# Hybrid decoder step: attention tiles taken in reverse with new phases, and folded mLSTM weights

## The reference

```python
u = rmsnorm(x, pre_g) @ w_in            # 28 column tiles: QA KA VA ZA XB OB ZB, 4 heads each
# differential attention, 4 heads, two maps of 64 dims in each head
w = softmax(q1 k1^T / 8) - lam * softmax(q2 k2^T / 8);  a = headnorm(w @ v) * silu(za)
# mLSTM, 4 heads of 128; xc is a causal conv of 4 taps over xb
xch = silu(xc); qb = xch @ wq; kb = xch @ wk * 128**-0.5; vb = xb @ wv
gates = concat(qb, kb, vb) @ w_if + b_if
# chunked scan, stabilised: C = decay*C + sum wg * k (x) v ; n likewise
h = (w_in * q C + (q k^T * wD) v) / max(|den|, exp(-m)) * sigmoid(ob)
bo = (headnorm(h) + skip * xch) * silu(zb)
y = concat(a, bo) @ w_out; x = x + rmsnorm(y); x = x + rmsnorm(sigmoid(x@ple_gate) * (p@ple_w))
```

## Time and profile before

| | us |
|---|---|
| median of 3 runs (1136.88 to 1139.03) | 1138.99 |
| the profiled execution, its own time | 1136.47 |
| its span, first to last instruction | 1134.8 |
| TensorE busy in the span | 1009.9 (89%) |
| VectorE busy | 514.7 (45%) |
| ScalarE busy | 419.9 (37%) |
| mean granted TensorE clock | 0.961 of 2.4 GHz |

### The profile page before, as it was taken

One profiled execution on the slowest core, in us unless ns is written; L12 is line 12 of the kernel. 1 busy time (PEld: TensorE's weight loads), 2 busy tenths in 40 slices (PEclk: granted clock), 3 DMA queues, 4 the chain that ended last, 5 costly groups with the idle time before them and its releaser, 6 DMA issues.

```text
span 1134.8 us, 19697 instructions
## 1 busy us (share of the span) xinstructions
PE 1009.9 (89%) x7424; PEld 802.3 (71%) x7424; DVE 514.7 (45%) x1196; ACT 419.9 (37%) x902; POOL 137.1 (12%) x289
## 2 busy tenths in 40 slices
PE   4789999999999999985889888888876999899997
PEld 4779989999888888864556555555545888577773
DVE  4523744554653444433655545455443434432222
ACT  4433253333245434342544343344435223321111
POOL 1300010000000000030022222222220000000000
PEclk9989999999999999987999999899996999999998
DMA  6351115111322222239677666566365322212210
GB/s 195 88 149 57 57 57 131 56 57 57 103 75 79 71 75 61 71 91 282 202 240 243 205 207 222 182 217 219 117 235 209 143 95 75 82 48 84 83 66 24
DMA packets 111305, 142.16 MB, mean 125 GB/s; under 512 B 9304, under 2 KB 75481, under 8 KB 111212
## 3 DMA queue, kind: packets, MB, share of 16 engines
q1 hardware_dynamic: 100972, 107.34, 30.0%
q0 software_dynamic: 10240, 33.56, 9.4%
HBM read 125.47 MB, written 15.41 MB: 124 GB/s over the span
## 4 chain that ended last, share of the span: by engine, by line
PE 78%; DVE 9%; ACT 4%; issue 3%; DMA 3%; POOL 2%; SPq 1%; POOLq 0%; ACTq 0%; DVEq 0%
PE ps L1632 65%; PE ps L1635 12%; DVE pp L1508 2%; DMA out_k_prompt<-ktok 1%; DMA wst<-in_w_in 1%; DVE kTs L1456 1%; DMA xrow<-in_x_prompt 1%; DVE st L1506 1%; DVE pp L1495 1%; DVE hrow L1070 1%; DVE wlo L1076 1%; PE ps L1627 1%; SPq L366 1%; POOL si L666 1%; ACT whi L710 1%
## 5 line engine op out<-in xcount | busy, mean ns | idle before, releaser
L1632 PE MATMUL ps<-hhi,whi 128*128 128x272 f32 (+1 forms) x672 | 228.4, 340 | 6.8 <-DVE wlo L1076 5.6
L1632 PE MATMUL ps<-hhi,wlo 128*128 128x272 f32 (+1 forms) x672 | 219.2, 326 | 0.0
L1632 PE MATMUL ps<-hlo,whi 128*128 128x272 f32 (+1 forms) x672 | 218.4, 325 | 0.0
L1632 PE MATMUL ps<-wh,r 128*128 128x512 f32 (+1 forms) x576 | 163.6, 401 | 4.3 <-DVE wout_lo L1574 4.3
L1632 PEld LDWEIGHTS ps<-hhi,whi 128*128 128x128 f32 x672 | 129.0, 192 | 18.3 <-DVE wlo L1076 5.9
L1632 PEld LDWEIGHTS ps<-hlo,whi 128*128 128x128 f32 x672 | 129.1, 192 | 10.0 <-issue 1.9
L1632 PEld LDWEIGHTS ps<-hhi,wlo 128*128 128x128 f32 x672 | 128.6, 191 | 9.3
L1632 PEld LDWEIGHTS ps<-wh,r 128*128 128x128 f32 (+1 forms) x576 | 103.9, 183 | 33.8 <-issue 4.6
L1076 DVE TENSOR_TENSOR wlo<-wst,whi 128x1024 fp32r<-128x1024 f32 x56 | 68.6, 1224 | 87.7 <-ACT whi L710 87.7
L653 POOL DMA_DIRECT2D Vr<-in_cache_v x128 | 69.8, 545 | 206.0 <-PE ps L1632 186.3
L1456 DVE COPY kTs<-ps 128x512 f32<-128x512 f32 x64 | 44.3, 692 | 106.3 <-PE ps L1635 106.3
(11 more groups left out here) (305 smaller groups left out, 1602.7 us busy)
## 6 DMA issues: line engine op xcount, KB each, us to landing
Kr<-in_cache_k SPq DMA_DIRECT2D x128, 256.0 KB, 3.1
Vr<-in_cache_v POOLq DMA_DIRECT2D x128, 256.0 KB, 3.7
wst<-in_w_in SPq DMA_DIRECT2D x56, 512.0 KB, 3.8
out_y_prompt<-rows SPq DMA_DIRECT2D x16, 512.0 KB, 2.9
xrow<-in_x_prompt SPq DMA_DIRECT2D x8, 512.0 KB, 3.6
wout<-in_w_out SPq DMA_DIRECT2D x4, 1024.0 KB, 12.7
rows<-in_x_prompt SPq DMA_DIRECT2D x8, 512.0 KB, 4.3
wgate<-in_ple_gate_w SPq DMA_DIRECT2D x2, 2048.0 KB, 10.7
```

What stands on the lines that cost most here:

```text
L1632: return nc.tensor.matmul(out, lhsT, rhs, start=start, stop=stop)
```

## The change

The attention units are taken from the last tile of queries to the first (`tile_of`), so that units 0 to 15 have two parts and the others one; the phases of every engine are laid out anew; both maps' scores wait for the row minima of both and signal once. Decode steps are given out by the new sizes, the last five of them over positions of units 30 to 32. `ktok` has eight buffers, placed where `pp` lies later; the SiLU of ZA moves between the key tiles, and the state and sample outputs behind the eighth. In the mLSTM q and k are no longer both made: wq wk^T is folded once (`wqk`), x stands in k's place in the scores and the state, and wk is applied to the state at the end. The gate weights are folded too (`wg`, 8 blocks of 36 columns), and v is projected token-major at once. `wqk` and `wg` are copied to the second half's buffers by DMA.

```diff
-PARTS = [-(-(u // H + 1) * P // PART) for u in range(UNITS)]
+PARTS = [-(-(CH - u // H) * P // PART) for u in range(UNITS)]
...
+BUSY_UNITS = UNITS - 2
-SHARES = CH * [2.0] + [(4 + u // H) / PHASES if u < UNITS else 0.0 for u in range(UNITS + 4) for _ in range(PHASES)]
+SHARES = CH * [2.0] + [(4 + CH - u // H) / PHASES if u < BUSY_UNITS else 0.0 for u in range(UNITS + 4) for _ in range(PHASES)]
...
+DECODED = [round((STEPS_OF_DECODE - 5) * sum(SHARES[:pos + 1]) / sum(SHARES))
+           + min(5, max(0, (pos - CH - BUSY_UNITS * PHASES) // 2)) for pos in range(POSITIONS)]
...
+ktok = place("ktok", [P, CH, 512], offset=u1_base + XB * HALF * 4)
```

SP and ACT around the key tiles, and ACT's phases:

```diff
-            sp.wait_ge(s["C_done"], CH)
-            put("out_state", io["C_prompt"][0, 0].rearrange("h d e -> d h e"), Caug[:, :, 0:DH])
...
-                    sp.dma_start(kp[pos * P:(pos + 1) * P, :], ktok[:, pos % 2, :]).then_inc(k_out[pos % 2], 16)
+                    sp.dma_start(kp[pos * P:(pos + 1) * P, :], ktok[:, pos, :]).then_inc(k_out[pos // H], 16)
...
                 if pos == CH - 1:
+                    sp.wait_ge(*done["state_stored"])
+                    put("out_state", io["C_prompt"][0, 0].rearrange("h d e -> d h e"), Caug[:, :, 0:DH])
...
-            gate_tiles(ZA, 0, ACT.Silu)
-            gate_tiles(ZA, 1, ACT.Silu)
-            nc.scalar.preload_act_table_set("natural_log_exp_and_others")
             act.wait_ge(s["bo_done"], CH)
+            act.wait_ge(*done["state_ready"])
+            for b in range(2):
+                last = nc.scalar.activation(Caug[:, 2 * b:2 * b + 2, :].rearrange("p h d -> p (h d)"), ps[:, 6 + b, 0:258], ACT.Copy,
+                                            scale=KSCALE)
...
             def keys_out(t):
                 act.wait_ge(s["kt_ready"], t + 1)
-                if t >= 2:
-                    act.wait_ge(k_out[t % 2], 16 * (t // 2))
-                copy(ktok[:, t % 2, :], ps[:, 4 + t % 2, :], "kt_stored")
+                copy(ktok[:, t, :], ps[:, 4 + t % 2, :], "kt_stored")
+                if t == 2:
+                    gate_tiles(ZA, 0, ACT.Silu)
+                if t == 3:
+                    gate_tiles(ZA, 1, ACT.Silu)
...
             def attend(u, phase):
-                if phase == 0 and u >= 6 and u % H == 2:
-                    heads_square(u // H - 1)
+                if phase == 0 and two(u - 2):
+                    weights_out(u - 2, 1)
                 if phase == 1 and u < UNITS and not two(u):
                     head_exp(u)
-                if phase == 1 and 1 <= u <= UNITS:
+                if phase == 2 and u >= 5 and u % H == 1:
+                    heads_square(u // H - 1)
+                if phase == 3 and 1 <= u <= UNITS:
                     weights_out(u - 1, 0)
-                if phase == 2 and two(u - 1):
-                    weights_out(u - 1, 1)
                 if phase == 3 and two(u):
                     head_exp(u)
```

DVE and PE in the merged stage (DVE's `attend` keeps `head_rows(u, 0)` in phase 0, `head_weights(u - 1)` in phase 1 and `head_rows(u, 1)` in phase 2; `heads_scale` moves to phase 0):

```diff
             def head_rows(u, c):
+                if u < 2 and c == 0:
+                    dve.wait_ge(k_out[u], 16 * H)
...
+                dve.wait_ge(s["score_pair"], pair + 1)
                 for m in range(2):
...
-                    dve.wait_ge(s["score_pair"], 2 * pair + m + 1)
...
             def head_scores(u, c):
+                if pair:
+                    pe.wait_ge(s["row_min"], 2 * pair)
                 for m in range(2):
-                    if pair:
-                        pe.wait_ge(s["row_min"], 2 * pair - 1 + m)
...
             def attend(u, phase):
                 if phase == 0:
-                    if u >= 7 and u % H == 3:
-                        heads_back(u // H - 1)
                     if two(u):
                         head_scores(u, 1)
                     elif u + 1 < UNITS:
                         head_scores(u + 1, 0)
-                if phase == 1 and 1 <= u <= UNITS:
+                if phase == 1 and 2 <= u < UNITS + 2:
+                    head_values(u - 2)
+                if phase == 1 and u >= 7 and u % H == 3:
+                    heads_back(u // H - 1)
+                if phase == 2 and 1 <= u <= UNITS:
                     head_turn(u - 1, 0)
-                if phase == 2:
+                if phase == 3:
+                    if two(u) and u + 1 < UNITS:
+                        head_scores(u + 1, 0)
                     if two(u - 1):
                         head_turn(u - 1, 1)
-                    if two(u) and u + 1 < UNITS:
-                        head_scores(u + 1, 0)
-                if phase == 3 and 2 <= u < UNITS + 2:
-                    head_values(u - 2)
```

PE in the mLSTM: the folding, once, and the chunk:

```diff
-            fill(4)
+            fill(2)
...
+            for bank, w in ((6, wq), (7, wkv[:, 0, :, :]), (4, wkv[:, 1, :, :])):
+                for h in range(H):
+                    last = turn(ps[:, bank, h * P:(h + 1) * P], w[:, h, :])
+            last.then_inc(*signal["weights_T"])
+            fill()
...
+            for h in range(H):
+                mm(ps[:, 5, h * P:(h + 1) * P], qbT[:, h, :], kbT[:, h, :])
+            for h in range(H):
+                mm(ps[:, 6, 8 * h:8 * h + 8], qbT[:, h, :], wif[:, 3 * h, :], True, False)
+                mm(ps[:, 6, 8 * h:8 * h + 8], kbT[:, h, :], wif[:, 3 * h + 1, :], False, True)
+            for h in range(H):
+                last = mm(ps[:, 6, 32 + 8 * h:40 + 8 * h], wvT[:, h, :], wif[:, 3 * h + 2, :])
...
             def chunk(i):
...
-                for j in range(3):
...
-                    for h in range(H):
-                        src = tok(XB + h, i * P, P) if j == 2 else xch[:, h, t0:t0 + P]
-                        last = mm(ps[:, 4 + j, h * P:(h + 1) * P], wqkv[:, j, h, :], src)
-                    last.then_inc(s["proj_ready"], 1)
+                for h in range(H):
+                    last = mm(ps[:, 5, h * P:(h + 1) * P], wqk[:, h, :], x[h])
+                last.then_inc(s["proj_ready"], 1)
+                for h in range(H):
+                    last = turn(ps[:, 4, h * P:(h + 1) * P], x[h])
...
+                for h in range(H):
+                    last = mm(ps[:, 6, h * P:(h + 1) * P], tok(XB + h, i * P, P), wkv[:, 1, h, :])
...
+                for g in range(2 * H):
+                    last = mm(ps[0:36, 7, 0:P], wg[:, g, :], x[g] if g < H else tok(XB + g - H, i * P, P),
+                              g == 0, g == 2 * H - 1)
+                last.then_inc(s["gates_ready"], 1)
                 fill(before_turn)
                 if i % H:
                     finish(i - 1)
                 fill(before_gates)
-                pe.wait_ge(s["qk_stored"], 2 * i + 2)
+                pe.wait_ge(s["qk_stored"], i + 1)
                 pe.wait_ge(s["v_stored"], i + 1)
-                for c in range(12):
-                    for n in range(2):
-                        last = mm(ps[32 * n:32 * n + H, 7, 0:P], wif[:, c, H * n:H * n + H], (qbT, kbT, vbT)[c % 3][:, c // 3, :],
-                                  c == 0, c == 11)
-                last.then_inc(s["gates_ready"], 1)
-                for bank, buf in ((4, kbT), (5, vbT)):
-                    for h in range(H):
-                        last = turn(ps[:, bank, h * P:(h + 1) * P], buf[:, h, :])
...
+                    last = mm(ps[:, 6, h * P:(h + 1) * P], x[h], qbT[:, h, :])
...
             pe.wait_ge(s["C_done"], CH)
             pe.wait_ge(s["bo_done"], CH)
+            for h in range(H):
+                last = mm(ps[:, 6 + h // 2, 129 * (h % 2):129 * (h % 2) + 129], wkv_[1][:, 0, h, :], Caug[:, h, :])
+            last.then_inc(*signal["state_ready"])
```

More of the change, by code:

```diff
@@ L198, in program @@
         half_buffers.append(chunk_buffers(1, base))
[L199 to L200 removed]
+        end_of_chunks = base + 33856
+        assert top[0] <= end_of_chunks
+        E_, nd_, vaug_, qbT_, kw_, Ablk_, gat_, G_, wqk_, wkv_, xch_, wg_ = (
             [b[name] for b in half_buffers]
[L202 removed]
+            for name in ("E", "nd", "vaug", "qbT", "kw", "Ablk", "gat", "G", "wqk", "wkv", "xch", "wg"))
+        wvT = kw_[0]
         top[0] = sample_base
@@ L239, in program @@
         mask_w = place("mask_w", [P, SEQ])
-        ktok = place("ktok", [P, 2, 512])
         pT = place("pT", [P, PAGES + 1, 32])
@@ L243, in program @@
         S = [None, place("S1", [P, PAST + SMP])]
+        kS = place("kS", [SMP, 512])
+        xbS = place("xbS", [SMP, 512])
         st = place("st", [P, 2 * H, 8])
@@ L246, in program @@
         assert top[0] <= end_of_chunks, top[0]
-        top[0] = base
-        kS = place("kS", [SMP, 512])
-        xbS = place("xbS", [SMP, 512])
-        xbP = place("xbP", [3, 512])
-        assert top[0] <= base + 2 * CH * P * 4
+        xbP = place("xbP", [3, 512], offset=base + 2 * CH * P * 4)
         top[0] = end_of_chunks
@@ L671, in _ @@
                 u, phase = divmod(pos - CH, PHASES)
-                if u >= 6 and u % H == 2 and phase == 0:
+                if u >= 5 and u % H == 1 and phase == 3:
                     heads_root(u // H - 1)
@@ L772, in _ @@
             copy(Cs[:, :, DH], ps[:, 5, 0:SMP], "n_stored")
```

(44 more changed lines are left out.)

211 lines of the change are left out of this document (111 added, 100 removed).

## The result

The changed kernel takes **1100.9 us** (median of 4 runs, 1100.1 to 1102.1) against 1138.2 for the kernel before (4 runs, 1136.9 to 1139.0): a ratio of 0.967, 95% interval 0.966 to 0.969. It is faster by 37 us, where 65 were forecast, and the 1100 at the top of the range just misses it. The profiled executions took 1136.5 and 1102.1 us, 34 us apart.

The account below looks back on a forecast made before the run. PE's own work was taken to bound the mLSTM, PE's waits the later stretches. 1136.5 - 13 (mLSTM) - 11 (transition) - 38 (merged stage) - 3 (end) = 1071.5, forecast 1072 us, range 1048 to 1100.

Parts of the forecast that it names:

- mLSTM, -13: mLSTM chunks: fewer projections, transposes and gate matmuls -18, folding products +3.6, new waits +1.5; -13 us (-6 to -17).
- The 1.5 us of new waits at `GT`: mLSTM chunks: PE reaches the gates' turn sooner than their chain; 1.5 us over 8 chunks, bounds 0 and 8.
- Transition, -13: Between mLSTM and merged stage: key stores no longer wait for DMA; 10.8 + 3.4 + 3 - 2 - 2 = 13 us saved.
- the two "- 2": Transition sum: two deductions of 2 us; about 2 us was named for new state products and evictions.
- The start of the merged stage, 2 us: First attention units: waits for key tiles' DMAs and small outputs issued before key pages lose 2 us (0 to 13).
- The step that failed: Merged stage: a phase between `head_weights` and `head_turn` removes PE's 37 us of waits on `pp`.
- The new wait, +13: Merged stage: `head_scores(u, 1)` waits for DVE's rows, 0.8 us in each of 16 two-part units, 13 us lost.
- The clock, -10: Merged stage: low clock falls around the long waits and costs 4 us in place of 14.
- Pairs, -4: Merged stage: score pairs that ran one behind the other run together, saving 4 us.
- The end, -3: Last units and output projection: work in front of the last waits and earlier `w_out` loads save 3 us (0 to 6).
- The first rival: Merged stage: `head_scores(u, 1)` waits a whole DVE pass per two-part unit; stage gives 12 us, 1098 us; chance 15%.
- The -55 of the merged stage: Merged stage, high end of the forecast -38: DVE runs ahead of PE and the new wait vanishes.

Follow-up runs that it names:

- the fold alone: The kernel before with only the mLSTM part of the change, merged stage and SP's order as before: 1127.4 us, ratio 0.988.
- after: The changed kernel with the whole change, against the kernel before: 1100.9 us, 0.967; once more 1107.1 us, 0.970.
- the best kernel: The changed kernel with small outputs ten positions later and the second block's scores a phase later: 1093.4 us, 0.960; once more 1092.1 us, 0.958.

## Why the prediction was wrong

- **mLSTM, -13: right, in part by luck.** 13.8 us by the trace, 13 by the fold alone. PE's busy time in the stretch fell by 12.6 us, where the sum has 14.4, and its idle time by 1.2, where it has 1.5 more: two misses that cancel. A chunk's projections, turns, `v` and gates take 4.2 us (368.30 to 372.48), where I had 4.0. The 1.5 us of new waits at `GT` did not come, and the row on `G`, 1.9 us before, is gone.
- **Transition, -13: right in kind, 3 us short.** `ktok` waits 1.5 us in place of 10.8. I had `xbS` as moved (3.4 us); it is 0.3 now. Idle time fell by 11.1 us. The other 4.7 are clock, which costs 1.7 us there in place of 6.4; the sum had no term for it. (In the sum one of the two "- 2" has no name; if it is the moved wait, that one is 3.4.)
- **The start of the merged stage, 2 us: wrong, and a part of the miss.** I named both mechanisms (the unit's rows behind `k_out`, some 17 issues in front of the next keys) and their end of the range, 13 us. The start idles for 13.8 us, 7.6 more than before; 3.9 of them stand behind `k_out` and 4.1 on keys, 8 together for the 2. The outputs later took the 4.1 away.
- **The step that failed** is the one that read: `head_turn` has a phase between it and `head_weights`, "so the 37 us go", with 13 us on `st` as all that comes in their place: 24 us of idle time saved. The row went (33 us), and `st` came (18.7). But 8.2 us on `S` and 5.6 on `on` came too, which no term held, and the idle time of the stage rose by 1.8 us. It was not the reversal that did it: in ascending order 27 us of the row went, and 1.0 of idle time. The same shows in single edits. The turn moved back: 11 us of the row, 4.5 of idle time. The second pair later: 16 us of `st`, 3.6 of idle time. The scaling earlier: 7 us of `on` gone, 5.6 of idle time more. A wait's row says where PE stood, not what would be saved. My account of it, argued and not shown by itself: PE, DVE and ACT hand each other one unit's rows, exponentials and weights, and in between the decode's keys, `S` and `pT`, each in a fixed order, so while PE stood for `pp`, DVE and ACT also caught up with everything else.
- **The new wait, +13: right in size, wrong as a limit.** In the steady part `st` stood 14.4 us in 16 waits, 0.9 each against my 0.8. In the rest of the stage it had 9 more.
- **The clock, -10: wrong.** I let it go with the waits. In the steady part it did (0.96 to 0.99), but the start fell from 1.00 to 0.82 and the end from 0.90 to 0.82: the clock costs 16.8 us where I gave 4. The Trainium skill's rule ("TensorE: Matmul & The Clock Gate", "A second HAM failure mode: psum-queue depth-cycling"), that frequent short idles between groups make the clock go down and up, is not borne out by this trace: 16 waits of 0.9 us in 196 us left it at 0.99 (0.97 in the second profile of after), and what fell was the start and the end, with waits of up to 4.1 and 4.6 us.
- **Pairs, -4: right in kind, the term mis-sized.** In the trace after, the two maps' score records of a pair start 5 to 8 ns apart in all but the first case; before, in 57 of 94 cases within 12 ns. PE's rows of scores (`ps<-U`, 64*128) sum to 53.2 us busy before and 46.0 after; at the full clock that is 49.4 and 40.5. So the pairs gave 9 us, not 4, and 9 of the 10 by which the stage's work fell (262.3 to 251.9). The 41 us that the sum of the work gives to all pairs side by side were right; the 4 did not follow from them.
- **The end, -3: wrong.** The last 97.4 us idle for 26.7 us, 24.1 before. One-part units with one or two steps leave PE at `on` (3.7 and 2.0 us) and the clock low.
- **The first rival** (the wait moves, 15%, 1098 us) came nearest in time. Its mechanism, a whole DVE pass in each unit, is not what happened: the wait was spread over several tiles.
- **The bounds.** The -55 of the merged stage is 4 us more than its terms give: with no new wait they are -37 - 10 - 4 = -51. It touches only the low end of the range.

What stays open: which of the hand-overs sets the 55 us of idle time that the best kernel keeps, and what `pp` in a place of its own would give at the start. Of added work, PE's own (32 us) left the idle time as it was, and 40 us on DVE added 15.

## What to carry to other kernels

Do not price a removed wait at its row. Price it by what is late next on every engine of that chain, or undo it alone once it is built: here 33 us of a row went and the idle time stayed, and 11 us of it put back were some 5 us of time. Split such a stage into work, idle time and clock, and look at its first and last tens of microseconds apart: steady numbers say nothing of a start with all outputs in front of the loads.

## What was not expected of the hardware

- The share of low clock is not a property of the kernel: two profiles of one program, with idle time and waits alike to 0.4 us, have a mean clock of 0.92 and 0.90 in the merged stage and lengths of 331.8 and 338.9 us. Sets of four to ten runs of one variant spread over 1 to 15 us (1099.2 to 1100.5 in one, 1086.2 to 1101.1 in another), all sets of the kernel before over 2 to 8. So comparisons of under 1% here need several sets of runs.
- What an output takes of SP's queue depends less on its size than on when it is issued. `n`, whose data is 2 KB, took 2.18 us to issue behind the last key tiles in after, and 0.51 in before, in ascending order and where the outputs were moved later. The same group of 14 issues took 10.0 us in after, 7.1 in before and 5.4 in the run with the outputs later. One of the eight pieces of 6 KB took about 0.4 us, a tile of 256 KB of keys on its way out 0.35 to 0.71.
